# Feed-forward layers: the seven-product section starts at the fifth pair and covers ten pairs, and its operands are made inside four dense pairs

## What is computed

```python
def rms_norm(x, g):
    y = x * rsqrt(mean(x * x, axis=-1) + 1e-6)
    return y * g

def swiglu(x, wi, wo):                 # wi: 1024 x 5632, wo: 2816 x 1024
    gate, up = split(x @ wi, 2, axis=-1)
    return (silu(gate) * up) @ wo

h = h + 0.5 * swiglu(rms_norm(h, ffn_norm), wi, wo)
```

## Time and profile before

| | |
|---|---|
| runs, median (lowest to highest of 3) | 2728.4 us (2726.09 to 2729.82) |
| the profiled execution's own time | 2729.47 us |
| its span in the trace | 2727.6 us |
| PE busy in the span | 2683.4 us (98%) |
| DVE, ACT, POOL busy | 1775.8, 1283.9, 893.2 us |
| mean granted TensorE clock | 0.997 |
| dense products L281 on the longest chain | 61% of the span |
| seven-product groups L978 on it | 12% |

### The profile page before, as it was taken

One profiled execution on the slowest core, in us unless ns is written; L12 is line 12 of the kernel. 1 busy time (PEld: TensorE's weight loads), 2 busy tenths in 40 slices (PEclk: granted clock), 3 DMA queues, 4 the chain that ended last, 5 costly groups with the idle time before them and its releaser, 6 DMA issues.

```text
span 2727.6 us, 40995 instructions
## 1 busy us (share of the span) xinstructions
PE 2683.4 (98%) x15550; PEld 2225.5 (82%) x15550; DVE 1775.8 (65%) x2625; ACT 1283.9 (47%) x2024; POOL 893.2 (33%) x751
## 2 busy tenths in 40 slices
PE   8999999999999999999999999999999999899998
PEld 6998888789888898887778998877888888777777
DVE  7874336569763587735965887348677777676664
ACT  4542232546332454223563542346655555467775
POOL 5520013136331254402733445013322222022232
PEclk9999999999999999999999999999999999999999
DMA  4342332223553325633203246322222222122222
GB/s 143 88 124 89 99 84 78 77 79 101 168 162 100 93 86 150 184 94 91 78 21 96 85 133 188 106 77 71 72 73 74 71 71 63 43 78 68 63 62 70
DMA packets 484875, 255.93 MB, mean 94 GB/s; under 512 B 17843, under 2 KB 478422, under 8 KB 484710
## 3 DMA queue, kind: packets, MB, share of 16 engines
q1 hardware_dynamic: 484534, 253.40, 32.5%
q10 hardware_dynamic: 176, 0.27, 0.0%
HBM read 251.51 MB, written 2.13 MB: 93 GB/s over the span
## 4 chain that ended last, share of the span: by engine, by line
PE 91%; DVE 5%; ACT 2%; issue 1%; POOL 1%; DMA 0%; SPq 0%; DVEq 0%; ACTq 0%; POOLq 0%
PE bank L281 61%; PE bank L978 12%; PE bank L2495 2%; PE bank L2526 1%; PE bank L2528 1%; PE bank L2527 1%; DVE w_lo L267 1%; DVE dsa_work L2191 1%; PE bank L3438 1%; PE bank L3430 1%; DVE small L2185 1%; PE bank L2639 1%; PE bank L3463 1%; DVE gdn_blocks L3032 1%; PE bank L1569 1%
## 5 line engine op out<-in xcount | busy, mean ns | idle before, releaser
L267 DVE TENSOR_TENSOR w_lo<-w_raw,w_hi 128x1024 fp32r<-128x1024 f32 x365 | 463.0, 1271 | 463.4 <-ACT w_hi L261 444.2
L281 PE MATMUL bank<-x_hi,w_hi 128*128 128x512 f32 x1808 | 737.9, 408 | 6.0 <-DVE w_lo L267 4.2
L281 PE MATMUL bank<-x_lo,w_hi 128*128 128x512 f32 x1808 | 707.7, 391 | 0.6 <-DVE x_lo L623 0.6
L281 PE MATMUL bank<-x_hi,w_lo 128*128 128x512 f32 x1808 | 707.6, 391 | 0.0
L261 ACT ACTIVATE w_hi<-w_raw 128x1024 fp32r<-128x1024 f32 x349 | 366.8, 1056 | 489.8 <-PE bank L281 441.0
L281 PEld LDWEIGHTS bank<-x_hi,w_hi 128*128 128x128 f32 x1808 | 340.4, 188 | 88.1 <-issue 15.7
L281 PEld LDWEIGHTS bank<-x_hi,w_lo 128*128 128x128 f32 x1808 | 340.1, 188 | 74.3
L281 PEld LDWEIGHTS bank<-x_lo,w_hi 128*128 128x128 f32 x1808 | 341.1, 189 | 68.1 <-DVE x_lo L623 3.8
L468 POOL TENSOR_TENSOR sumsq<-sumsq,sq 128x512 f32<-128x512 f32 x56 | 90.3, 1613 | 714.0 <-ACT sq L456 713.5
L281 PE MATMUL bank<-h_hi,w_hi 128*128 128x512 f32 x768 | 300.3, 391 | 0.0
L281 PE MATMUL bank<-h_hi,w_lo 128*128 128x512 f32 x768 | 299.0, 389 | 0.0
(11 more groups left out here) (541 smaller groups left out, 5067.2 us busy)
## 6 DMA issues: line engine op xcount, KB each, us to landing
w_raw<-in_ffn_wi_dram SPq DMA_DIRECT2D x176, 512.0 KB, 3.8
w_raw<-in_ffn_wo_dram SPq DMA_DIRECT2D x64, 512.0 KB, 3.6
w_raw<-in_ada_w_dram SPq DMA_DIRECT2D x48, 512.0 KB, 4.8
w_raw<-in_a_w_in_dram SPq DMA_DIRECT2D x48, 512.0 KB, 4.0
w_raw<-in_b_w_in_dram SPq DMA_DIRECT2D x32, 512.0 KB, 4.1
w_raw<-in_ffn_wo_dram SPq DMA_DIRECT2D x32, 384.0 KB, 3.1
w_raw<-in_even_w_in_dram SPq DMA_DIRECT2D x16, 512.0 KB, 4.0
w_raw<-in_a_w_out_dram SPq DMA_DIRECT2D x16, 512.0 KB, 3.5
```

Of the source, the lines that this page charges most:

```text
L267: dve.tensor_tensor(w_lo[s][:], w_raw[raw_of(b) % RAW][:], w_hi[s][:].bitcast(F32), ALU.subtract).then_inc(w_lo_done, 1)
L281: mm = pe.matmul(out, lhs[:, w], rhs(kt), start=first and kk == 0 and m == 0, stop=last and kk == len(kts) - 1 and m == 2)
```

## The change

The section starts two pairs earlier and is two pairs longer (`SEVEN_AT` 4, `SEVEN_N` 10), so pairs 0 to 3 are dense, 4 to 13 are in the section, 14 to 21 are dense. `seven_act` and `seven_dve` now begin with pair 2, and the loop of ordinary turns ahead of them runs once. DVE makes all eight pieces of `x_part` in pair 0: four ahead of `split_lo` of block 3 and four behind it, both ahead of the first gate. All four `part_act` stand in `seven_act` behind pair 1, and `part_dve` 0 to 3 are spread over pairs 2 and 3. `own_dve` 3 stays at n = 3. The waits that keep `h_hi` off quarters still being read move to the section's n = 1 and n = 5. POOL makes the second pair's `w_both` ahead of the first pair's low and all sums, with one more wait. The columns of `h_hi` and `h_lo` that each pair uses are the same as before (`seven_col`).

```diff
--- before.py
+++ after.py
@@ -44,7 +44,7 @@
 OUT3 = 3
 
 SEVEN = (0, 1, 2, 3)
-SEVEN_AT, SEVEN_N, OWN_LAST = 6, 8, 3
+SEVEN_AT, SEVEN_N, OWN_LAST, OWN_FIRST = 4, 10, 5, 1
 HT = T // 2
 FFN_B, FFN_T = 2 * FT + OUT3 * KT, 2 * FT + KT
 GLA_P = 17
@@ -112,7 +112,7 @@
 
 def seven_col(n):
 
-    return {SEVEN_AT - 2: 12, **{SEVEN_AT - 1 + k: 4 + (4 + k) % 8 for k in range(8)}}.get(n, n)
+    return {SEVEN_AT: 12, **{SEVEN_AT + 1 + k: 4 + (4 + k) % 8 for k in range(8)}}.get(n, n)
 
 
 def first_and_second_block(nc, a, out):
@@ -796,9 +796,6 @@
                         split_hi(act, b0 + o0 + 2 * s + 1 + AHEAD, i, 4, raws)
 
                     split_hi(act, b0 + o0 + 2 * s + 2 + AHEAD, i, 4, raws)
-                    if ahead and turn0 and s:
-                        part_act(act, f, 0)
-                        part_act(act, f, 1)
                     act.wait_ge(prod_done, pair + i * 2)
                     act.activation(h_hi[:, col(i * 2 + 2 * turn0 + s)], prod[s][:], ACT.Copy).then_inc(h_hi_done, 1)
             split_hi(act, b0 + AHEAD)
@@ -821,7 +818,12 @@
                 for s in range(2):
                     pair = FT * f + 2 * turn0 + s + 1
                     o = o0 + 2 * s
+                    early = f in SEVEN and turn0 == 0 and s == 0
+                    if early:
+                        parts_dve(dve, f, gain, range(4))
                     split_lo(dve, b0 + o + AHEAD, i, 4)
+                    if early:
+                        parts_dve(dve, f, gain, range(4, KT))
                     if ada:
                         ada_multiply(dve, f, 2 * s, i)
                     dve.wait_ge(block_done, SPLIT + b0 + o + 1 + i * 4)
@@ -836,10 +838,6 @@
                     dve.wait_ge(silu_done, pair + i * 2)
                     dve.wait_ge(tile_free, BANKS + t0 + o + 2 + i * 4)
                     dve.tensor_tensor(prod[s][:], prod[s][:], gate_s[s][:], ALU.mult).then_inc(prod_done, 1)
-                    if f in SEVEN and turn0 == 0:
-                        parts_dve(dve, f, gain, range(4 * s, 4 * s + 4))
-                    if f in SEVEN and turn0 == 1 and s:
-                        part_dve(dve, f, 0)
                     dve.wait_ge(h_hi_done, pair + i * 2)
                     h = col(i * 2 + 2 * turn0 + s)
                     dve.tensor_tensor(h_lo[:, h], prod[s][:], h_hi[:, h].bitcast(F32), ALU.subtract).then_inc(h_ready, 1)
@@ -1109,8 +1107,8 @@
 
         def seven_h_hi(act, f, n):
             act.wait_ge(prod_done, seven_pair(f, n))
-            if n == OWN_LAST:
-                act.wait_ge(own_lo, 4 * SEVEN.index(f) + 4)
+            if n in (OWN_FIRST, OWN_LAST):
+                act.wait_ge(own_lo, 4 * SEVEN.index(f) + (3 if n == OWN_FIRST else 4))
             act.activation(h_hi[:, col(seven_col(SEVEN_AT + n))], prod[(SEVEN_AT + n) % 2][:], ACT.Copy).then_inc(h_hi_done, 1)
 
         def next_hi(act, f, k):
@@ -1132,9 +1130,9 @@
 
             def high(s):
                 act.wait_ge(prod_done, pair + s)
-                if s == 1:
-                    act.wait_ge(own_lo, 4 * SEVEN.index(f) + 3)
                 act.activation(h_hi[:, col(seven_col(SEVEN_AT - 2 + s))], prod[s][:], ACT.Copy).then_inc(h_hi_done, 1)
+            part_act(act, f, 0)
+            part_act(act, f, 1)
             part_act(act, f, 2)
             part_act(act, f, 3)
             silu(0)
@@ -1260,18 +1258,19 @@
                 dve.wait_ge(h_hi_done, pair + s)
                 dve.tensor_tensor(h_lo[:, h], prod[s][:], h_hi[:, h].bitcast(F32), ALU.subtract).then_inc(h_ready, 1)
             split_lo(dve, b0 + 2 * SEVEN_AT - 1)
+            part_dve(dve, f, 0)
             gate(0)
             part_dve(dve, f, 1)
+            part_dve(dve, f, 2)
             up(0)
             product(0)
             left_dve(dve, f, 0)
-            part_dve(dve, f, 2)
             low(0)
+            part_dve(dve, f, 3)
             gate(1)
             both_dve(dve, f, 0)
             row_dve(dve, f, 0)
             own_dve(dve, f, 0)
-            part_dve(dve, f, 3)
             up(1)
             both_dve(dve, f, 1)
             own_dve(dve, f, 1)
@@ -1296,7 +1295,7 @@
                     dve.sem_inc(w_lo_done, 2 * SEVEN_N)
                     split_lo(dve, seven_block(f, SEVEN_N))
                 all_dve(dve, f, n)
-                if n == OWN_LAST:
+                if n == OWN_LAST - 2:
                     own_dve(dve, f, 3)
                 up_dve(dve, f, n - 1)
                 if n + 2 < SEVEN_N:
@@ -1322,6 +1321,7 @@
             pool.wait_ge(*loaded(raw + 1))
             if n:
                 pool.wait_ge(both_lo, c)
+                pool.wait_ge(three_added, c)
             pool.tensor_tensor(w_both[:], w_raw[raw % RAW][:, LEFT_H], w_raw[(raw + 1) % RAW][:, LEFT_H], ALU.add).then_inc(both_added, 1)
 
         def three_pool(pool, f, n):
@@ -1345,12 +1345,13 @@
 
         def seven_pool(pool, f):
             parts_pool(pool, f)
-            for n in range(2):
-                both_pool(pool, f, n)
-                three_pool(pool, f, n)
-                low_pool(pool, f, n)
-                if n == 0:
-                    all_pool(pool, f, 0)
+            both_pool(pool, f, 0)
+            three_pool(pool, f, 0)
+            both_pool(pool, f, 1)
+            low_pool(pool, f, 0)
+            all_pool(pool, f, 0)
+            three_pool(pool, f, 1)
+            low_pool(pool, f, 1)
             for n in range(SEVEN_N - 1):
                 all_pool(pool, f, n + 1)
                 if n + 2 < SEVEN_N:
```

## The result

| | before | after |
|---|---|---|
| median of the runs (6 each) | 2727.24 us | 2748.61 us |
| the profiled execution's own time | 2729.47 us | 2748.7 us |
| its span | 2727.6 us | 2746.9 us |
| PE busy | 2683.4 us | 2684.5 us |
| DVE, ACT, POOL busy | 1775.8, 1283.9, 893.2 us | 1826.9, 1301.6, 941.5 us |

The changed kernel is slower: ratio 1.0075, 95% interval 1.0064 to 1.0087. The forecast was 2749.0. One of the six runs of the changed kernel took 14895.6 us; the ratio leaves it out, and without it the median is 2748.51.

What follows compares the result with a forecast made beforehand. PE bounds the kernel, busy 98% of the span, and would now wait for DVE. Three parts at +4.1 (12.3) plus part 0 at +8.5 give +20.8, so 2749 us; range 2733 to 2755.

Steps and rivals of the forecast that it cites:

- The gain: On PE, two pairs of 48 matmuls of 512 columns become two of 84 of 256: 1.6 us per part saved.
- The shared port: DVE instructions with two SBUF operands and POOL sums exclude each other; a 1024-wide sum holds about 2.2 us.
- The budget: From `rstd` to the first product: DVE 26.8 us plus POOL 12.1, less at most 4.2, into 35.4.
- The walk of part 1: DVE and POOL timed from `rstd` on: added waits 5.5 to 5.9 us, net +4.1 per part.
- The tail of the walk: After the first product: waits 0.3 at second seventh product, 0.8 at row product (n=1), 0.6 at seventh (n=2).
- Part 0: First feed-forward part: 2.6 at block 3, 4.2 at seventh product, then 1.95 and 1.4, less 1.6: +8.5.
- The clock falls too: Rival: two halts of about 4 us in part 0 lower PE's clock, +1.7 to +3.4, 2751 to 2753; chance 0.12.
- The rule weighed: The `x_part` pieces on DVE hold the port against POOL's sums; if they left it free, +15.4 instead of +20.8.
- Sharing better than walked: Rival: POOL's sums fall beside DVE's bank reads: 2724.6, chance 0.11; with part 0 covered too, 2722, chance 0.06.
- DVE first whenever ready: Rival: DVE keeps the port when ready; about +2.6 per part, +8 in part 0: 2744, chance 0.15.
- The half case: Rival: waits in part 0 as walked, parts 1 to 3 about even: +8.5, 2737; chance 0.11.
- Edits at nothing: SP's earlier loads, ACT's waits for `own_lo` and POOL's added wait cost nothing.

Runs made afterwards that it cites:

- Experiment 1: Changed kernel, but POOL adds only 32 of each 256 columns of the four 1024-wide sums in parts 1 to 3; 2732.65 us, ratio 1.0016.
- experiment 6: Changed kernel with POOL's sums in the order from before the change, without the added wait; 2752.66 us, ratio 1.0087.
- experiment 3: Changed kernel with four `x_part` pieces behind the product of pair 0 and four behind that of pair 1; 2748.68 us, ratio 1.0072.
- experiment 2: Changed kernel with all eight pieces of `x_part` behind block 3's split, in every part; 2751.76 us, ratio 1.0085.
- experiment 5: Changed kernel with `own_dve` 0 ahead of `row_dve` 0 and `own_act` 0 ahead of its neighbours; 2747.71 us, ratio 1.0070.

## Why the prediction was right

- **The gain: 1.6 us per part.** Experiment 1 shows 1.56 to 1.63. Right.
- **The shared port.** Right, and shown by experiment 1: with POOL's four sums narrow, all new waits of parts 1 to 3 are gone. The budget was 34.7 to 38.9 us into 35.4. `own_dve` 0 ends at 605.51, 39.4 us after `rstd` and 4.0 past the 35.4, which is the four waits up to there (0.35, 1.20, 0.62 and 1.77). It is the upper end of the budget and a little more, but not because POOL's sums kept off the bank reads. DVE's lengthened rows add up to 10.2 us, so some 2 of POOL's 12.1 did fall beside something else. What the budget left out is 1.8 us in which DVE stood still, most of it twice 0.70 for ACT's `h_hi`.
- **The walk of part 1.** Moved by the 8.16 us by which `rstd` is later, it had block 4's split done at 578.3, block 5's at 585.1, `both_dve` 0 at 602.0 and `own_dve` 0 at 605.4. The rows have 578.37, 585.13, 602.15 and 605.51. One turn came out otherwise: the walk has the fifth piece go ahead of POOL's first sum, and the trace has that piece wait for it (2.89). It changes nothing behind it. The waits forecast were 0.3 to 0.7, 1.3, 0.6 and 1.95; measured 0.35, 1.20, 0.62 and 1.77.
- **The tail of the walk was mis-sized.** It gave 0.8 at the row product of n = 1 and 0.6 at the seventh of n = 2. Measured: 0.64 and less than 0.25. All in all the changed kernel loses 5.2 us per part against experiment 1, not 5.5 to 5.9, so the net is +3.6 and not +4.1.
- **Part 0** was forecast at +8.5 and came to +8.13, but its terms came out otherwise. Block 3's +2.6 is right (1.55 to 4.15). The seventh product was to be 4.2 late and the first 1.95; measured 2.74 and 0.66. The rest went to slower matmuls. In block 3 nine distances between matmuls take 3.65 us (42.25 to 45.90) in place of 2.04, 1.6 more, and the twelve of the seventh product are 0.21 apart in place of 0.12, 1.1 more. With these it is 4.3 and 1.8. The starts that DVE sets came as walked: the seventh at 73.4 against 72.8. That the total comes within 0.4 is partly luck, since the same code took 1.05 more in experiment 1.
- **"The clock falls too"** was half right. It fell, twice, but the +1.7 to +3.4 didn't follow. The step that failed was to add it to the waits: PE was not the limit there. Part 0 shows that a fall need not cost time, and experiment 6 that it can. The Trainium skill (TensorE: Matmul & The Clock Gate, Part 1) has the clock drop to half when the engine is found idle; by that rule the trace agrees, with 0.50 at 74 to 76 behind a wait of 2.74. The wait alone doesn't tell whether it falls: see experiments 3 and 6.
- **Block 3's wait as a term of its own.** It is one in the sum, but not one that could be taken away: experiment 2 removed it, and part 0 took 145.58, no less than the 144.54 and 145.59 that it takes with it.
- **The rule weighed.** That the pieces L913 (L911 now) hold the port was taken from one row of a similar instruction. The row of 4.88 shows it: four pieces that take 2.74 alone, with a sum beside them. The Trainium skill (GPSIMD Engine Reference, Key points) says that DVE contends with GpSimd when it has two SBUF inputs; the trace agrees, with 2.14 us.
- **The other rivals fell.** Sharing better than walked would have had `own_dve` 0 done by 601.4. DVE first whenever ready would have left blocks 4 and 5 on time. The half case would have had parts 1 to 3 even.
- **Edits at nothing:** no transfer appears among the waits of PE in part 1, and none for `own_lo` among ACT's. Right. (POOL's first `w_both` did wait for a transfer, until 589.19, but its low part was made in turn at 601.55.)

The sum: forecast +20.8; by the parts +18.9, by the two medians +21.4.

## What to carry to other kernels

Before moving work ahead on an engine, add up its queue between the two fixed points, and add every instruction of the other engine that shares its memory port; and the times in which the queue must wait for others; if that sum meets the time between the points, the order within the queue mostly chooses where the waiting stands. Ask for the largest step that still has cover: one more pair gained 0.8 us in each of parts 1 to 3 by the traces, two lost 3.6. Busy shares don't show it (65% and 33% over the whole span here); the stretch between the two points and the lengths of single instructions do.

## What I had not expected of the hardware

- A sum of POOL costs DVE nearly the same whether it meets one instruction or a row of them: 2.14 more on four pieces (4.88 against 2.74), 1.83 more on one split (3.04 against 1.21). It takes one turn on the port and is done; DVE is not slowed at an even rate, for of those four pieces one took 2.89 and the others 0.74.
- A wait of 2.19 us brought the clock to 0.50 in part 3 of experiment 6. In its part 1, after a wait of 2.16 at the same place, the clock was 1.00 in every stretch from 606 to 616. In experiment 3 a wait of 2.9 brought it down in parts 1 and 2 and not in part 3. What sets them apart stays open.
- A fallen clock cost nothing where another engine set the pace (part 0 of the changed kernel: 3.26 against 3.27 us between the same two starts), and 1.9 us where PE did (part 3 of experiment 6), with 0.4 to 0.7 in experiments 3 and 5.
